# Second expert rows are joined to the first ones on GpSimd, ahead of VectorE's pass over the stream

## The reference

```python
lg = xf @ w_rg + b_rg
grp = argmax(lg);  p_grp = softmax(lg)[grp]
top_v, top_i = top_k(le[grp], 2)
gate = p_grp * softmax(top_v)                  # two gates per token
y = (silu(xb @ w_gate[e]) * (xb @ w_up[e])) @ w_down[e]
h = h + gate[0] * y_first + gate[1] * y_second
```

## Time and profile before

| | |
|---|---|
| median of 3 runs | 1596.91 us (1595.47 to 1598.76) |
| the profiled execution | 1596.78 us, its span 1595.0 us |
| PE busy | 1368.2 us, 86% of the span |
| DVE busy | 404.1 us, 25% |
| ACT busy | 314.9 us, 20% |
| POOL busy | 190.4 us, 12% |
| mean granted TensorE clock | 0.955 of full speed |
| L1709, first pass over h | 9 times, median 1.279 us |
| L1257, diagonal products, tail | 16 matmul records, 7.9 us busy |

### The profile page before, as it was taken

The page is one execution under the profiler, slowest core; times in us unless marked ns, Lnnn a source line. Parts: engine busy times, 40 slices in busy tenths (PEclk is TensorE's granted clock), DMA queues, the critical chain, the costliest instruction groups (busy, mean ns, idle before and its releaser), DMA issues. The chain is left out here.

```text
span 1595.0 us, 17848 instructions
## 1 busy us (share of the span) xinstructions
PE 1368.2 (86%) x6820; PEld 767.4 (48%) x6820; DVE 404.1 (25%) x763; ACT 314.9 (20%) x605; POOL 190.4 (12%) x309
## 2 busy tenths in 40 slices
PE   5999996999888887877999878896998888788787
PEld 4999774333322232223789656784333323233232
DVE  3434424000000000003635688524000000000003
ACT  5212221111100000002532366330111000000002
POOL 2000001111111111111000000001111111111111
PEclk9999996999999999999999989997999999999999
DMA  9130446999999999997423210445999999999995
GB/s 344 52 107 1 159 158 240 386 426 423 426 426 426 426 426 426 424 425 308 131 69 118 74 45 1 159 190 214 403 426 424 425 427 426 426 424 423 427 423 219
DMA packets 63099, 473.75 MB, mean 297 GB/s; under 512 B 11232, under 2 KB 11308, under 8 KB 38976
## 3 DMA queue, kind: packets, MB, share of 16 engines
q1 hardware_dynamic: 48656, 442.55, 67.5%
q0 software_dynamic: 14384, 30.36, 5.1%
HBM read 465.17 MB, written 23.13 MB: 306 GB/s over the span
## 5 line engine op out<-in xcount | busy, mean ns | idle before, releaser
L1104 PE MATMUL ps<-ring,act 128*64 128x512 f32 x1792 | 443.9, 649 | 77.3 <-DMA ring<-in_e_up 63.6
L1104 PEld LDWEIGHTS ps<-ring,act 128*64 128x64 f32 x1792 | 141.7, 142 | 374.2 <-issue 374.2
L1651 DVE TENSOR_TENSOR act<-act,ps 128x256 f32<-128x256 f32 x64 | 26.9, 421 | 871.3 <-ACT act L888 871.3
L1127 PE MATMUL ps<-ring,act 128*64 128x512 f32 x896 | 204.6, 597 | 31.0 <-ACT act L890 31.0
L1069 PE MATMUL ps<-parts 128*128 128x512 f32 x576 | 143.2, 408 | 8.6 <-DVE parts L1447 7.7
L1042 PE MATMUL ps<-parts 128*128 128x264 f32 x1152 | 144.4, 287 | 4.5 <-DVE parts L1439 2.9
L1042 PEld LDWEIGHTS ps<-parts 128*128 128x128 f32 x1152 | 143.0, 191 | 5.5 <-issue 5.5
L888 ACT ACTIVATE act<-ps 128x256 f32<-128x256 f32 x64 | 24.6, 384 | 558.9 <-PE ps L1104 558.9
L1127 PEld LDWEIGHTS ps<-ring,act 128*64 128x64 f32 x896 | 70.8, 136 | 126.2 <-issue 126.2
L1069 PEld LDWEIGHTS ps<-parts 128*128 128x128 f32 x576 | 111.2, 196 | 37.3 <-issue 6.4
L1320 PE MATMUL ps<-parts 128*128 128x264 f32 (+1 forms) x576 | 92.4, 322 | 1.2 <-PE ps L1320 0.9
(11 more groups left out here) (209 smaller groups left out, 1066.8 us busy)
## 6 DMA issues: line engine op xcount, KB each, us to landing
ring<-in_e_gate SPq DMA_DIRECT2D x56, 2048.0 KB, 17.6
ring<-in_e_up SPq DMA_DIRECT2D x56, 2048.0 KB, 22.3
ring<-in_e_down SPq DMA_DIRECT2D x56, 2048.0 KB, 22.3
arena<-in_e_down SPq DMA_DIRECT2D x8, 2048.0 KB, 16.1
ring<-in_a_w_in SPq DMA_DIRECT2D x6, 2048.0 KB, 19.7
arena<-in_e_up SPq DMA_DIRECT2D x6, 2048.0 KB, 18.9
arena<-in_e_gate SPq DMA_DIRECT2D x6, 2048.0 KB, 14.0
ring<-in_w_kv SPq DMA_DIRECT2D x4, 2048.0 KB, 13.4
```

What stands on the lines that cost most here:

```text
L1104: last = mm(ps[f * C:(f + 1) * C, 2 + b, :].rearrange("p (g m i) -> p g m i", g=2, i=2), x, w, start=(k == 0), stop=(k == KC - 1))
L1127: last = mm(ps[o * C:(o + 1) * C, 6 + b, :], hT[:, b, (2 * c + a) * C:(2 * c + a + 1) * C], w[:, f * D + o * DH:f * D + (o + 1) * DH], sta ...
```

## The change

GpSimd now works on tiles 1 and up in both layers. When a tile's rows have landed, it multiplies the second rows by `ratio` (e1, kept in its own small tensor) in place, waits for that, and adds them to the first rows, in place. VectorE waits for `joined` and needs one pass, because gate0 * (y0 + e1 * y1) is gate0 * y0 + gate1 * y1. Tile 0 stays with VectorE, with two passes in both layers now. `by_product`, `second_gate`, their four operations on VectorE in layer 1's routing and the diagonal products on TensorE go. One small copy of e1 comes into the routing of both layers. At the end of the program VectorE's order becomes: combine 0, take_last 0, combine 1, take_last 1, combine 2, finish 0, take_last 2, combine 3, finish 1, take_last 3, finish 2, finish 3.

```diff
+        ratio = sb("ratio", [P, NX + 1])
...
-        def by_product(layer, t):
-            return layer == 1
-        def second_gate(t):
-            return nat[:, 1, DH + t * P:DH + (t + 1) * P]
...
 # GpSimd, behind the loop that issues the DMAs of all tiles
+                for t in range(1, nt):
+                    pool.wait_ge(y_landed[layer][t], 32)
+                    nc.gpsimd.tensor_scalar(y_in(t, 1), y_in(t, 1), ratio[0:rows(t), t:t + 1], None, ALU.mult).then_inc(weighed_in, 1)
+                    pool.wait_ge(weighed_in, NX * layer + t)
+                    nc.gpsimd.tensor_tensor(y_in(t, 0), y_in(t, 0), y_in(t, 1), ALU.add).then_inc(joined, 1)
...
 # TensorE, add_last
-                both = by_product(layer, t)
-                if both:
-                    pe.wait_ge(gates_ready, NX)
-                    pe.wait_ge(y_landed[layer][t], 32)
-                    for a in range(2):
-                        mm(last_rows(layer, t)[:, a, :], second_gate(t), y_in(t, 1)[:, a * DH:(a + 1) * DH], start=True, stop=False)
                 pe.wait_ge(y_ready, E * (layer + 1))
                 for a in range(2):
-                    last = mm(..., start=not both, stop=True)
+                    last = mm(..., start=True, stop=True)
...
 # VectorE, routing
+                order(v.tensor_copy(ratio[:, 0:nt], e1))
...
-                for t in range(nt):
-                    if by_product(layer, t):
-                        v.tensor_scalar(second_gate(t), ident, gate[:, 1, t:t + 1], None, ALU.mult).then_inc(gates_ready, 1)
...
 # VectorE, combine
-                dve.wait_ge(y_landed[layer][t], 32)
+                if t:
+                    dve.wait_ge(joined, NX * layer + t)
+                else:
+                    dve.wait_ge(y_landed[layer][t], 32)
                 order(v.scalar_tensor_tensor(h[0:r, t, :], y_in(t, 0), gate[0:r, 0, t:t + 1], h[0:r, t, :], ALU.mult, ALU.add))
-                if not by_product(layer, t):
+                if t == 0:
                     order(v.scalar_tensor_tensor(h[0:r, t, :], y_in(t, 1), gate[0:r, 1, t:t + 1], h[0:r, t, :], ALU.mult, ALU.add))
...
 # VectorE, the end of the program
-            for t in range(NX - 1):
-                combine(1, t)
+            combine(1, 0)
             for t in range(NX):
                 take_last(1, t)
-                if t == 0:
-                    combine(1, NX - 1)
-                else:
+                if t < NX - 1:
+                    combine(1, t + 1)
+                if t:
                     finish(t - 1)
             finish(NX - 1)
```

More of the change, by code:

```diff
@@ L334, in build @@
         zero_ready, zeroed = sem("zero_ready"), sem("zeroed")
-        gates_ready, weighed_in = sem("gates_ready"), sem("weighed_in")
+        joined, weighed_in = sem("joined"), sem("weighed_in")
         last_marked, last_turned, last_placed, last_done = sem("last_marked"), sem("last_turned"), sem("last_placed"), sem("last_done")
@@ L1250, in add_last @@
             def add_last(layer, t):
-                both = by_product(layer, t)
-                if both:
-                    pe.wait_ge(gates_ready, NX)
-                    pe.wait_ge(y_landed[layer][t], 32)
-                    for a in range(2):
-                        mm(last_rows(layer, t)[:, a, :], second_gate(t), y_in(t, 1)[:, a * DH:(a + 1) * DH], start=True, stop=False)
                 pe.wait_ge(y_ready, E * (layer + 1))
                 for a in range(2):
-                    last = mm(last_rows(layer, t)[:, a, :], last_gate(t)[a * C:(a + 1) * C, :], last_y[a * C:(a + 1) * C, :], start=not both, stop=True)
+                    last = mm(last_rows(layer, t)[:, a, :], last_gate(t)[a * C:(a + 1) * C, :], last_y[a * C:(a + 1) * C, :], start=True, stop=True)
                 last.then_inc(last_done, 1)
```

## The result

The changed kernel takes 1605.84 us (median of 6 runs, 1603.14 to 1608.12), the one before in the same rounds 1596.19 (1593.63 to 1598.76). The ratio is 1.0067, its 95% interval 1.0053 to 1.0081: slower, by 8.5 to 12.9 us. The forecast was 1604.8.

A forecast was written before the change was run, and what follows sets the result against it. Transfers bound the expert stages; the change touches two seams of some 15 us, after layer 0 and at the end. 1596.8 + 3.3 (seam after layer 0) + 4.7 (tail) = 1604.8 us, routing 0; range 1597 to 1611.

The forecast's parts named there:

- The weighing: GpSimd's product of a tile's second rows by ratio: 1.06 us, from the slope of its copies; up to 2.5.
- The sum: GpSimd's addition of a tile's two row sets: 1.95 us, operands read in turn; ends 1.06 to 3.4.
- The wait between: GpSimd's wait for its own semaphore between its two operations on a tile: 0.3 us, ends 0.1 and 0.88.
- Exclusion: VectorE operations with two SBUF inputs and GpSimd's reading ones wait for each other's whole operation; chance 0.60.
- The copy at 17.25: Profile row taken as sign of a hold: GpSimd's 128x32 copy beside a VectorE tensor_tensor took 0.73 us, later 0.21.
- The tail: Last combining and scaling after layer 1's experts: last scaling ends 4.7 us later, ends +1.7 and +9.1.
- rival A: Engines work side by side: seam -1.3 us, tail +1.9, so no change, 1597.4 us; chance 0.22.
- Rival B: Engines side by side but a GpSimd sum of 3.4 us: seam +0.1, tail +5.7, 1602.6 us; chance 0.12.
- The seam: Adding expert rows to h after layer 0: take_last 1 comes 3.3 us later, ends +1.1 and +6.2.
- Only the time at which tile 1 is taken counts: After layer 0, TensorE waits 4.02 us for take_last 1 and then for no later tile.
- Routing: One added copy (0.17 to 0.20 us), four VectorE products gone: set to 0, between -0.2 and +0.4 us for both layers.
- Rival C: A shorter TensorE wait after layer 0 spares its clock dip: 0.9 us beside the 1.3 saved, 1594.6 us; chance 0.03.

The follow-up runs named there:

- The probe: Kernel before, with GpSimd and VectorE operations of 128x1024 added behind its last scaling, alone and in pairs; alone, a copy took 1.04 us, weighing by a constant 2.77.
- the run of layer 1 alone: The change made in layer 1 only, layer 0 keeping its code of before; ratio 1.0054 to the kernel before.
- the run of layer 0 alone: The change made in layer 0 only, layer 1 keeping its code of before; ratio 1.0024 to the kernel before.
- the other weighing: The whole change, but GpSimd weighs by a product of two tensors, the second the ratio's column repeated; ratio 1.0100 to the kernel before.
- the two versions that gave TensorE work: Kernel before without GpSimd's help, diagonal product added for tile 1 of layer 0, dropped for tile 0 of layer 1; two orders, ratios 0.9991 and 0.9999.

## Why the prediction was right

The number, the sign and the range held; of the steps some did not, and that the number came so close is in part luck.

- **The weighing: 1.06 us forecast, 2.85 measured.** This term is mis-sized by 1.8 us for each of seven tiles. The copy's slope was the wrong neighbour: the copy itself is 1.04 at this width, as worked out, but a product by a column is another operation. The upper end, 2.5, was still too low.
- **The sum: 1.95 forecast, 2.34 measured**; the estimate from the Trainium skill (GPSIMD Engine Reference, § 3.1) was 2.25. **The wait between: 0.3 forecast, 0.09 measured** (1582.41 to 1582.50). A tile costs GpSimd 5.3 us instead of 3.4.
- **Exclusion: right that it exists and in both directions, wrong in its length.** The copy at 17.25 was no first call but a hold: the same first copy takes 0.21 us in four other profiles, in which it begins when VectorE's two-input operation is over, and 0.99 or 1.18 in two in which it begins 0.29 and 0.11 us behind that operation. GpSimd shuts VectorE out for 0.92 of 2.85 and 2.14 of 2.34 us. The Trainium skill (SBUF — State Buffer, § Who interferes with whom) calls the ports that VectorE and GpSimd share an exclusive lock, and says of VectorE's faster mode with two ports that whoever issues first has them for the whole instruction. The probe agrees to 0.13 us for GpSimd behind VectorE, and for which VectorE operations are hit (two SBUF inputs, and tensor_scalar, which that section counts among those with such a mode); for VectorE behind GpSimd it doesn't, and the measurement decides.
- **The tail: +4.7 forecast, +6.3 and +7.2 measured, and for another main reason.** By rival A's working, 2.8 of the 4.7 us were the exclusion's. With the measured durations the same working gives +7.2 for GpSimd's pace alone and +8.0 with the measured holds (an estimate: the sequence of the forecast with 2.85, 2.35, 0.92 and 2.14 put in). It ends the changed kernel's tail at 1603.1 from its own landings, where 1603.0 was measured, and the hold that reaches the end, the last sum's 0.6 us, is in the trace. So in the tail as it is the pace costs about 7 us and the holds under 1; with the pace shortened, as in the run in which ScalarE weighs, the holds are most of the 4.3 us by the same working, which has 1.5 for the pace alone. The two errors, a weighing too short and a hold too long, made up for each other, which is luck. Rival B had this kind of answer, a GpSimd dearer than the copies say, but put the price on the sum.
- **The seam: +3.3 forecast, all of it a later take_last 1.** Against the run of layer 1 alone, whose seam has the old code, take_last 1 came 3.1 us later in the changed kernel and 3.2 in the run of layer 0 alone; the seams are 2.9 and 4.2 us longer (2.4 and 3.7 against the profile before). The sequence was other than worked out: VectorE's piece was held for 0.5 us, not 1.6, and the idle 2.99 us ahead of the pass came from the long weighing.
- **"Only the time at which tile 1 is taken counts" held for the waits but left out TensorE's clock.** Beside take_last 1 and TensorE's part the seam has the same 16.2 to 16.3 us in every profile, but TensorE's part took 8.1 to 9.3 us with GpSimd at work in layer 0 and 11.7 with the other weighing. GpSimd moved take_last 1 even without work on tile 1 (+0.7), by holding a pass.
- **Routing: 0 forecast, 0 measured.** From VectorE's first operation of layer 1's routing to the first scaled expert input it is 20.7 us before, 20.7 with layer 1's change alone and 20.6 in the changed kernel.
- **Rival C's dip of the clock is real and worth 1.2 us** (7.02 against 5.81 for 24 products). That the change made it worse isn't shown: TensorE waits 7.1 us instead of 4.0, and yet its part of the seam is 8.1 us in the changed kernel, 8.3 before; it is 9.3 and 9.2 in the two other profiles with GpSimd at work only in layer 0. The saving was there in the two versions that gave TensorE work.

In the tail the change could gain nothing from the start: VectorE had one pass per tile already, TensorE's diagonal products were done before VectorE asked, and of tile 0 a pass came back.

## What to carry to other kernels

Before work goes to an idle engine, ask whose time the end depends on, and price the operation on its new engine by a row of that very operation: a copy of the same shape was off by a factor of 2.7. Here an elementwise helper on GpSimd beside VectorE was paid for by its pace, and could be by holds of VectorE's two-input operations too, wherever in the code they stand; a hold costs only where something waits for the held operation. Of two ways to do a step on GpSimd, the one that shuts VectorE out for less time can give the faster kernel, though it takes longer itself (2.85 against 1.89 us).

## What the runs showed of the hardware

- GpSimd, 128x1024 float32: copy 1.04 us, product by a column 2.85, by a constant 2.77, sum or product of two tensors 2.34, product with a repeated column 1.89.
- A GpSimd operation shuts out VectorE's operations with two SBUF inputs, and its tensor_scalar, from its start for 0.92 us (product by a column), 1.69 (with a repeated column) or 2.14 us (sum): less than its length in each case. An operation with one input in PSUM wasn't held (1.22 us). VectorE's passes shut out GpSimd's reading operations until 0.13 us before their end.
- An operation on 16 partitions costs GpSimd as much as one on 128: in layer 0 alone the sum of the meta tile takes 2.38 us, the others 2.36.
- TensorE's granted clock behind a wait wasn't fixed by the wait: from 758 to 764 it was 0.50 in the run of layer 0 alone, behind a wait of 7.24 us, and 0.82 in the changed kernel, behind one of 7.13.
